# A transformer pair in one fp32 kernel: where the gate projections and two reloads stand in the order

## What is computed

```
h = rmsnorm(x);  proj = h @ w_in
o_a = 8 heads of a gated delta rule on conv(q,k,v), both directions, times silu(z)
o_b = 3 groups of dilated window attention (4 heads each), merged by softmax of their log-sums
gate_a, gate_b = sigmoid of the last 2 x 1024 columns of proj
x = x + rmsnorm((gate_a * (o_a @ w_branch_a) + gate_b * (o_b @ w_branch_b)) @ w_out)
x = x + rmsnorm(relu(h2 @ w_ff1)^2 @ w_ff2), h2 = rmsnorm(x);  then the second layer
```

## Time and profile before

| what | us |
|---|---|
| median of 3 runs | 3851.43 (3847.93 to 3856.25) |
| profiled execution | 3857.1 |
| its span, first to last instruction | 3855.3 |
| PE busy | 3463.6 (90%) |
| delta stages 2 to 13, two stages (one head) | 156.9 each |
| stage 14, stage 15 | 50.4, 48.9 |
| attention of the last group | 71.4 |

### The profile page before, as it was taken

One profiled execution on the slowest core, in us unless ns is written; L12 is line 12 of the kernel. 1 busy time (PEld: TensorE's weight loads), 2 busy tenths in 40 slices (PEclk: granted clock), 3 DMA queues, 4 the chain that ended last, 5 costly groups with the idle time before them and its releaser, 6 DMA issues.

```text
span 3855.3 us, 36936 instructions
## 1 busy us (share of the span) xinstructions
PE 3463.6 (90%) x15359; PEld 2460.1 (64%) x15359; DVE 1408.4 (37%) x2051; ACT 963.4 (25%) x2238; POOL 329.5 (9%) x425
## 2 busy tenths in 40 slices
PE   6999989899898799999977998999999868698997
PEld 4455655556556547585753486777777656477786
DVE  3344444444444300101012333444444545532453
ACT  2332233232323211202120022111111123211452
POOL 0121222111222100000001000000000000000211
PEclk9999999999999899999998999999999968898898
DMA  3111011110110010101023222111111220010100
GB/s 124 50 52 42 22 39 39 44 39 23 50 31 31 7 62 31 44 14 55 33 100 150 90 93 77 54 44 44 53 47 44 73 78 33 19 50 23 55 28 33
DMA packets 51863, 194.67 MB, mean 50 GB/s; under 512 B 7136, under 2 KB 10720, under 8 KB 38640
## 3 DMA queue, kind: packets, MB, share of 16 engines
q1 hardware_dynamic: 49680, 187.03, 13.8%
q10 hardware_dynamic: 2016, 5.28, 0.4%
HBM read 158.30 MB, written 33.98 MB: 50 GB/s over the span
## 4 chain that ended last, share of the span: by engine, by line
PE 78%; DVE 10%; ACT 6%; DMA 2%; issue 2%; POOL 1%; ACTq 0%; SPq 0%; DVEq 0%; POOLq 0%
PE ps L509 14%; PE ps L1358 9%; PE ps L1956 9%; PE ps L1957 8%; PE ps L1958 8%; PE ps L1383 5%; PE ps L1671 4%; PE ps L1849 3%; PE ps L572 2%; PE ps L578 2%; DVE ar L940 2%; PE ps L2728 1%; PE ps L1433 1%; DVE r L1949 1%; ACT r L1944 1%
## 5 line engine op out<-in xcount | busy, mean ns | idle before, releaser
L509 PE MATMUL ps<-ar 128*128 128x512 f32 x1472 | 726.3, 623 | 48.6 <-DMA ar<-wst 24.4
L1956 PE MATMUL ps<-r,r 128*128 128x512 f32 (+3 forms) x1296 | 482.2, 372 | 61.8 <-DVEq L161 37.5
L1957 PE MATMUL ps<-r,r 128*128 128x512 f32 (+3 forms) x1296 | 467.4, 361 | 0.0
L1958 PE MATMUL ps<-r,r 128*128 128x512 f32 (+3 forms) x1296 | 466.5, 360 | 0.0
L509 PEld LDWEIGHTS ps<-ar 128*128 128x128 f32 x1472 | 268.8, 200 | 273.3 <-issue 224.9
L1358 PE MATMUL ps<-ar 128*128 128x512 f32 x832 | 369.9, 595 | 0.0
L1956 PEld LDWEIGHTS ps<-r,r 128*128 128x128 f32 (+1 forms) x1296 | 256.2, 198 | 104.6 <-DVEq L161 38.8
L1957 PEld LDWEIGHTS ps<-r,r 128*128 128x128 f32 (+1 forms) x1296 | 255.8, 197 | 40.0 <-issue 6.6
L1958 PEld LDWEIGHTS ps<-r,r 128*128 128x128 f32 (+1 forms) x1296 | 255.3, 197 | 35.0
L1358 PEld LDWEIGHTS ps<-ar 128*128 128x128 f32 x832 | 154.5, 191 | 169.2 <-issue 168.5
L1956 PE MATMUL ps<-r 128*128 128x512 f32 x512 | 204.8, 400 | 20.5 <-DVE ar L2125 19.1
(11 more groups left out here) (312 smaller groups left out, 4613.4 us busy)
## 6 DMA issues: line engine op xcount, KB each, us to landing
ar<-wst SPq DMA_DIRECT2D x102, 1024.0 KB, 4.9
ar<-sc_g SPq DMA_DIRECT2D x32, 256.0 KB, 4.7
sc_h<-ar SPq DMA_DIRECT2D x32, 256.0 KB, 2.0
sc_x<-ar SPq DMA_DIRECT2D x16, 512.0 KB, 2.6
ar<-sc_x SPq DMA_DIRECT2D x16, 512.0 KB, 4.1
sc_b<-ar SPq DMA_DIRECT2D x24, 260.0 KB, 2.1
ar<-sc_b SPq DMA_DIRECT2D x3, 2080.0 KB, 19.9
ar<-x ACTq DMA_DIRECT2D x8, 512.0 KB, 18.0
```

Of the source, the lines that this page charges most:

```text
L509: o = t.do.matmul(bk, wv[:, kt, c:c + 128], hT[:, kt, 512 * hf:512 * hf + 512], start=(kt == 0), stop=(kt == 7))
L1956: t.do.matmul(o, l[0], r[0], start=first, stop=False)
L1957: t.do.matmul(o, l[0], r[1], start=False, stop=False)
L1958: return t.do.matmul(o, l[1], r[0], start=False, stop=last)
```

## The change

Gate blocks are computed with heads 1 to 4 (blocks 0 to 3), as `fill` beside stages 14 and 15 (blocks 4 and 5), and beside the last dilated group (blocks 6 and 7, 8 pieces in 17 steps instead of 4 in 9). Heads 5 to 7 have none. The weights of a head now stand in the order gate, qk, vz. In the last dilated group SP loads oT instead of mT; mT is loaded in four pieces after the last tile's store, in front of the engines' meeting; mT and oT trade places in memory, and x1 stays on oT's place, so that two later buffers wait for x1's last store.

```diff
+        GATES = [1, 2, 3, 4, 8, 9]
+        gate_of = lambda h: [(h, s, hf) for s in ("g0", "g1") for hf in range(2)]
+        halves = [(h, s, hf) for h in heads for s, hf in (PREPG if h in GATES else PREP)] + gate_of(8) + gate_of(9)
...
             if s < 14:
-                threads.append((("prep%d" % part, h + 1), NPREP + 8, 0.0, 1.0))
+                threads.append((("prep%d" % part, h + 1), NPREP + 8 * (h + 1 in GATES), 0.0, 1.0))
+            else:
+                threads.append((("fill", 8 + part), 16, 0.0, 1.0))
...
+        W_ORDER = [(w_, h) for h in heads for w_ in (["gate"] if h in GATES else []) + ["qk", "vz"]] + [("gate", 8), ("gate", 9)]
...
+        def pe_fill(t, h):
+            yield from pe_proj(t, h, "g0")
+            yield from pe_proj(t, h, "g1")
...
+        def act_fill(a, h):
+            for s in ("g0", "g1"):
+                for hf in range(2):
+                    yield from idle(3)
+                    act_gate(a, h, s, hf)
+                    yield
...
         def dve_prep0(v, h):
-            yield from idle(16 if h else 8)
+            yield from idle(16 if h in GATES else 8)
...
+        def sp_fill(sp, h):
+            yield from sp_gate(sp, h, "g0")
+            yield from sp_gate(sp, h, "g1")
...
-        gb_keys = [("gb", ct, hf) for ct in range(2) for hf in range(2)]
+        gb_keys = [("gb", c, ct, hf) for c in range(2) for ct in range(2) for hf in range(2)]
...
-                    merged((("att", 2), 34, 0.0, 1.0), (("gb", 3), 9, 0.0, 1.0))]
+                    merged((("att", 2), 34, 0.0, 1.0), (("gb", 3), 17, 0.0, 1.0))]
...
-        mT = A(R + 8192, 8, 1024)
+        mT, oT = A(R, 8, 1024), A(R + 8192, 8, 1024)
...
             sp.wait_ge(att_mm, (1, 7, "u"))
-            sp.do.dma_start(mT, sc_h[0:8].rearrange("a p n -> p a n")).then_inc(*ga_in.tick(0))
+            sp.wait_ge(o_saved[0], 6)
+            sp.wait_ge(o_saved[1], 7)
+            sp.do.dma_start(oT, sc_o.rearrange("a p n -> p a n")).then_inc(*oa_in.tick(0))
...
+            sp.wait_ge(att_mm, (2, 7, "s"))
+            for cb in range(4):
+                sp.do.dma_start(mT[:, 2 * cb:2 * cb + 2, :], sc_h[2 * cb:2 * cb + 2].rearrange("a p n -> p a n")).then_inc(*ga_in.tick(cb))
...
-            sp.wait_ge(o_saved[0], 6)
-            sp.wait_ge(o_saved[1], 7)
-            sp.do.dma_start(oT, sc_o.rearrange("a p n -> p a n")).then_inc(*oa_in.tick(0))
...
-        x1 = A(R, 8, 1024)
+        x1 = A(R + 8192, 8, 1024)
...
+                    a.wait_ge(x_saved, (1, 7))
                     a.do.activation(FT[s_], bank(s_), ACT.Relu).then_inc(*ff1_act.tick(("relu", *k)))
```

More of the change, by code:

```diff
@@ L344, in program @@
         PREPG = [("g0", 0), ("g0", 1)] + PREP[:6] + [("g1", 0), ("g1", 1)] + PREP[6:]
-        halves = [(h, s, hf) for h in heads for s, hf in (PREPG if h else PREP)]
-        gate_parts = [(h, s, hf) for h in heads[1:] for s in ("g0", "g1") for hf in range(2)]
+        GATES = [1, 2, 3, 4, 8, 9]
+        gate_of = lambda h: [(h, s, hf) for s in ("g0", "g1") for hf in range(2)]
+        halves = [(h, s, hf) for h in heads for s, hf in (PREPG if h in GATES else PREP)] + gate_of(8) + gate_of(9)
+        gate_parts = [k for h in GATES for k in gate_of(h)]
         gate_saved = [flow(f"gate_saved{q}", gate_parts[q::2], 16) for q in range(2)]
@@ L448, in program @@
         KQ = ps[:, 1024:2048].rearrange("p (j t n) -> p j t n", j=4, t=2)
+        W_ORDER = [(w_, h) for h in heads for w_ in (["gate"] if h in GATES else []) + ["qk", "vz"]] + [("gate", 8), ("gate", 9)]
+        W_AT = {(w_, GATES.index(h) if w_ == "gate" else h): n for n, (w_, h) in enumerate(W_ORDER)}
         def w_of(h, s):
             if s in ("g0", "g1"):
-                return 3 * h + 1, 128 * (s == "g1")
-            return (3 * h - 1 if h else 0) + (s in "vz"), 128 * (s in "kz")
+                return W_AT["gate", GATES.index(h)], 128 * (s == "g1")
+            return W_AT["vz" if s in "vz" else "qk", h], 128 * (s in "kz")
         def gate_row(h, s):
-            return 2 * (h - 1) + (s == "g1")
+            return 2 * GATES.index(h) + (s == "g1")
         def pe_gates(t):
@@ L522, in pe_prep0 @@
         def pe_prep0(t, h):
-            if h:
+            if h in GATES:
                 yield from pe_proj(t, h, "g0")
@@ L657, in make @@
                     return both(pe_prep0(t, 0), pe_prep1(t, 0))
-                return {"gates": pe_gates, "prep0": pe_prep0, "prep1": pe_prep1, "inv": pe_inv, "scan": pe_scan, "fin": pe_fin, "bias": pe_bias, "qk": pe_qk}[what](t, *of)
+                return {"gates": pe_gates, "prep0": pe_prep0, "prep1": pe_prep1, "inv": pe_inv, "scan": pe_scan, "fin": pe_fin, "bias": pe_bias, "qk": pe_qk, "fill": pe_fill}[what](t, *of)
             for order in plan:
@@ L883, in make @@
                     return both(act_prep0(a, 0), act_prep1(a, 0))
-                return {"gates": act_gates, "prep0": act_prep0, "prep1": act_prep1, "inv": act_inv, "scan": act_scan, "fin": act_fin, "bias": act_bias, "qk": act_qk}[what](a, *of)
+                return {"gates": act_gates, "prep0": act_prep0, "prep1": act_prep1, "inv": act_inv, "scan": act_scan, "fin": act_fin, "bias": act_bias, "qk": act_qk, "fill": act_fill}[what](a, *of)
             for order in plan:
@@ L964, in dve_prep1 @@
             yield from conv_steps(v, h, "k", chk[q])
-            yield from idle(12 if h else 4)
+            yield from idle(12 if h in GATES else 4)
             for n, _ in enumerate(conv_steps(v, h, "v", vf)):
@@ L1080, in make @@
                     return both(dve_prep0(v, 0), dve_prep1(v, 0))
-                if what in ("bias", "qk"):
+                if what in ("bias", "qk", "fill"):
                     return idle(1)
@@ L1090, in pool_prep1 @@
         def pool_prep1(p, h):
-            yield from idle(17 if h else 9)
+            yield from idle(17 if h in GATES else 9)
             p.wait_ge(unit_v, (h, "eps"))
@@ L1157, in make @@
                     return both(idle(NPREP), pool_prep1(p, 0))
-                return idle(1) if what in ("gates", "prep0", "bias", "qk") else {"prep1": pool_prep1, "inv": pool_inv, "scan": pool_scan, "fin": pool_fin}[what](p, *of)
+                return idle(1) if what in ("gates", "prep0", "bias", "qk", "fill") else {"prep1": pool_prep1, "inv": pool_inv, "scan": pool_scan, "fin": pool_fin}[what](p, *of)
             for order in plan:
@@ L1233, in make @@
                     return both(sp_prep0(sp, 0), sp_prep1(sp, 0))
-                return idle(1) if what == "scan" else {"gates": sp_gates, "prep0": sp_prep0, "prep1": sp_prep1, "inv": sp_inv, "fin": sp_fin, "bias": sp_bias, "qk": sp_qk}[what](sp, *of)
+                return idle(1) if what == "scan" else {"gates": sp_gates, "prep0": sp_prep0, "prep1": sp_prep1, "inv": sp_inv, "fin": sp_fin, "bias": sp_bias, "qk": sp_qk, "fill": sp_fill}[what](sp, *of)
             for order in plan:
@@ L1271, in program @@
         DIL = (1, 4, 8)
-        QK0, VW0, GB0 = 23, 27, 41
+        QK0, VW0, GB0 = 22, 26, 40
         def chunks(g):
@@ L1307, in program @@
         dil_ev = flow("dil_ev", dil_keys)
-        gb_saved = flow("gb_saved", gb_keys, 16)
-        ga_in = flow("ga_in", [0], 16)
+        gb_saved = [flow(f"gb_saved{q}", gb_keys[q::4], 16) for q in range(4)]
+        ga_in = flow("ga_in", range(4), 16)
         tile_list = [(g, i) for g in range(3) for i in range(len(tiles(g)))]
@@ L1438, in pe_gb @@
             for key in gb_keys:
-                yield from pe_cols(t, key, GB0, key[1], key[2])
+                yield from pe_cols(t, key, GB0 + key[1], key[2], key[3])
         def pe_dilated(t):
@@ L1518, in act_gb @@
                 a.wait_ge(att_mm, (1, 7, "u"))
-                a.do.activation(gbst[i], bank(dil_ev.keys.index(key) % 2), ACT.Tanh, scale=0.5).then_inc(*dil_ev.tick(key))
+                if i >= 4:
+                    a.wait_ge(gb_saved[i % 4], gb_keys[i - 4])
+                a.do.activation(gbst[i % 4], bank(dil_ev.keys.index(key) % 2), ACT.Tanh, scale=0.5).then_inc(*dil_ev.tick(key))
         def act_dilated(a):
@@ L1626, in program @@
         cb_in = flow("cb_in", range(3), 16)
-        oa_in = flow("oa_in", [0], 16)
         cb_exp_in = flow("cb_exp_in", range(3))
@@ L1784, in sp_branches @@
                 sp.do.dma_start(CBt[g], sc_b[g].rearrange("(i p) n -> p i n", p=P)).then_inc(*cb_in.tick(g))
-            sp.wait_ge(gb_saved, gb_keys[-1])
+            for q in range(4):
+                sp.wait_ge(gb_saved[q], gb_keys[4 + q])
             def gate_load(i):
@@ L3093, in stream @@
     for h in range(8):
+        if 1 <= h <= 4:
+            s.append(cols(w_in, gates[h - 1]))
         s.append(cols(w_in, 128 * h, 1024 + 128 * h))
         s.append(cols(w_in, 2048 + 128 * h, 3072 + 128 * h))
-        if h:
-            s.append(cols(w_in, gates[h - 1]))
+    for j in (4, 5):
+        s.append(cols(w_in, gates[j]))
     for g in range(3):
@@ L3101, in stream @@
                 s.append(cols(w_in, base + 512 * g + 256 * j))
```

(3 more changed lines are left out.)

19 lines of the change are left out of this document (11 added, 8 removed).

## The result

| what | before | after |
|---|---|---|
| median, us | 3851.74 (3847.93 to 3856.25, 4 runs) | 3800.18 (3795.23 to 3805.0, 4 runs) |
| profiled execution; its span | 3857.1; 3855.3 | 3799.06; 3797.3 |

The ratio is 0.9866, 95% interval 0.9849 to 0.9883: 51.6 us less, where 51.1 were forecast.

The account below looks back on a forecast made before the run. TensorE was taken to bound the kernel, carrying 78% of the chain. Terms -61.5 - 15.6 + 21.6 + 2.4 + 2 = -51.1 us took the median from 3851.4 to 3800, range 3772 to 3830.

Parts of the forecast that it names:

- stalls: Heads 2 to 4: PE's wait for gate weights and half-speed work behind it go, 5.2 us a head, -15.6 us.
- stages 8 to 13: Heads 5 to 7 without gate steps: even stages 67.1 us, odd 69.3, together -61.5 us.
- branch start: After the last tile: oT's wait goes but nothing is gained; PE idles in one piece, half-speed start adds +2 us.
- last group: Last dilated group with twice the gate pieces: 73.8 us against 71.4, +2.4 us.
- The chosen doubling of the v convolution: Odd stages 8 to 13: v convolution costs 4 us, chosen as twice its 1.9 because its cover is thinner.
- the clock taken as half of now: Stages 8 to 13: clock loss chosen as half of now, 1.7 us in even stages, 1.9 in odd.
- Rival 3: Stages 8 to 13 bound by the levels' own chain, only stalls go: -5.2 us, 3846, no change; chance 0.07.
- rival 2: Stages 8 to 13: gaps covered after all, even 60.1, odd 58.6 us; in all -104, 3747; chance 0.06.
- rival 4: Stages 8 to 13: idler PE drops the clock to 0.79, +75 us, 3875; chance 0.05.
- Stages 14 and 15: 16 gate steps put beside each stage: +12.1 us and +9.5 us, together +21.6.
- No tile waits: Last dilated group: tile 0's late store delays nobody, as the third tile's exponents are ready before its transposes.
- MLP: MLP part: the new wait for a store and the moved row load cost nothing, 0 us.

Follow-up runs that it names:

- e1: Kernel before with only the weight blocks reordered to gate, qk, vz, gates staying with heads 1 to 7: 3816.87 us, ratio 0.9908.
- e6: Changed kernel with one DVE convolution instruction moved a step earlier in the q and v convolutions of heads 5 to 7: 3780.0 us, ratio 0.9817.
- e2: Changed kernel with the two 4 MB loads put back, gate rows beside the last dilated group, oT behind the meeting: 3800.13 us, ratio 0.9867.
- e4: Changed kernel with four branch products, on PE and DVE, in front of the attention merge's first step: 3779.86 us, ratio 0.981.
- e3: Changed kernel with three result buffers for the attention tiles instead of two: 3792.92 us, ratio 0.9846.
- e5: Kernel before with four branch products in front of the attention merge's first step: 3852.33 us, ratio 0.9999.
- e7: Changed kernel with four branch products first and, in DVE's list alone, each merge step's sums two products earlier: 3769.77 us, ratio 0.9788.
- e8: Kernel before with four branch products first and, in DVE's list alone, each merge step's sums two products earlier: 3837.69 us, ratio 0.9969.

## Why the prediction was right, and where its terms were not

The time was right to 0.5 us, and so close a hit is luck. By the timed runs the order of the weights gave 34.3 (forecast 31.2 for six heads), the moved gates 16.7 (21.9), the loads 0 (2 lost): the errors cancel. By stages of the profile three terms gained more than forecast (stalls 4.2, stages 8 to 13 6.7, branch start 2.1) and one cost more (last group 6.8). Together they come to 6.9 more than forecast, and the distance of the two profiled runs from their medians is 6.4.

**Stalls, -15.6: mechanism and size right at the stall.** From `L603` to kq heads 2 to 4 gained 14.7 together (14.2 to 14.7 us each before, 9.57 after), 5.0 a head in e1. The profile of after has 19.8 up to stage 8, since less ran at half speed behind other waits, as in e1.

**Stages 8 to 13, -61.5: right in kind, 6.7 too small in this profile.** The even stage takes 65.9 (forecast 67.1), the odd 67.2 (69.3), stage 8 69.2; the three even ones together make 201.1 against 201.3, so the surplus is in the odd ones.

In the even stage the waits and the clock were overrated: `L590` and `L596` wait 0.2 to 0.7 each, and the clock is 1.00 in stages 10 and 12, where 1.7 us were counted. PE's own work was underrated, 59.3 busy against 56.9.

In the odd stage the wait for the first level is 4.0 + 1.4, against 7.0, gaps are 2.3 against 3.8, the v convolution costs one wait of 2.0, not the 4 that were chosen. Against that, bank waits are 2.6 for 1 and the clock of 0.95 costs 3.4 for 1.9. (Two sums of the prediction are off: the steps to the first level make 16.5, not 16.0, and the items of the even stage 67.2.) The chosen doubling of the v convolution and the clock taken as half of now were the weak steps. That the q and v convolutions are a cost at all is shown by e6.

The surplus itself may be chance: e2 runs the same code there, has the same waits to 0.1 us, and takes 408.0 us, where the changed kernel takes 402.6 and e4 399.4; its clock is 0.95 for their 0.97. By e2's profile the term is -62.8, against -61.5 forecast. Rival 3 (46 us less gain) and rival 2 (gaps covered, 60.1 and 58.6) are refuted by the same windows, rival 4 by their clock of 0.95 to 1.00.

**Stages 14 and 15, +21.6:** measured 21.0. The clock of stage 15 rose from 0.79 to 1.00.

**Last group, +2.4: the step that failed.** "No tile waits" was checked for the third tile's transposes only. What is late is the second tile's product, by way of ACT's list. e3 shows it: without that wait the group takes 74.1, against 73.8 forecast. The trace of before had the same sign: the 8.65 there also stood in front of `L1433`, released by `L1506`. How large the term is depends on the profile of before, whose group holds a second wait of 3.95 for `L1506`; in e5's trace of the same code that one is 1.79 and the group takes 67.0, not 71.4.

**Branch start, +2: right that nothing is gained, and why.** e2 shows that the load alone is worth 0; e4, e5, e7 and e8 show that the order of the lists turned its worth into another wait. One reason given was wrong: PE does not fill four banks. In 13.97 us it makes two products (a product is x16, one bank), and the 26.70 stand in front of its own transposes `L1715`, not of a product. DVE's list was a limit as well; e4 moves both lists, and no run moves PE's alone. The 2 us for the clock did not come.

The Trainium skill ("DMA: Bandwidth & Descriptors", rules for kernel authors: issue early, compute, wait late) holds here only where the wait for the data is the last one to end. The traces agree with it once the lists follow (16.5 us in e7 against e8), and not where the load alone is issued early (0 in e2), since PE's transposes and DVE's first line still waited for a later transfer.

**MLP, 0:** from the first transposes on 1792.6 us against 1792.5.

## What to carry to other kernels

An early load is worth what the lists of the other engines can do in the freed time: follow each list to its next wait before a gain is booked, and reorder those lists with it. A big load in front of small stores in one queue makes buffers late; look for the next user of each buffer on every in-order list, not only for the next instruction of the waiting engine. Moving filler work pays by the difference of two prices. 82.6 us of projections (48 steps of 1.72) taken out of stages 8 to 13, where PE was nearly full, gave about 53 (68.2 less three stalls of 5.0). 55 us of them put beside stages 14 and 15 cost 21, and the other 27.5 beside the last group cost 9 (3 with the third buffer).

## What was not expected of the hardware

The same 387 matmul instructions at the program's start took 143.2 us at a granted clock of 0.94 in one run and 136.6 at 0.99 in another, in kernels that are the same up to there. Of the eleven profiled runs three took 136.6 to 136.8 us up to there (e1, e6, e8), the others 142.6 to 143.8. The same code in stages 8 to 13 took 399.4 us in e4 and 408.0 in e2. So differences of 5 to 9 us between two profiles of one stretch say nothing by themselves.

DVE's 128x512 sums took 1.41 us each while POOL's product (`L1807`, eight in 9.78 us) ran, and 0.69 after it.
